# Seven products for eight in the second block's projections and in the dense layer's down products

## The chip, the cores and the metric

The kernel runs on one core of a Trainium2 chip. The metric is the device time of one execution in microseconds. The time before is 3156.32 us, the median of 3 runs (3151.3 to 3162.45).

## The reference, cut to what matters

Two blocks run one after the other on 512 tokens of width 1024, all in float32. The first block (a hybrid mixer and 16 experts) isn't touched. The second block has two layers; 16 meta tokens go ahead of the 512, so 528 rows. Each layer projects its input once, attends in a sliding window, convolves, mixes, and ends in a feed-forward part: a dense SwiGLU in the first layer, experts in the second.

```python
u = h @ w_in[i]                        # 528 x 1024 by 1024 x 3840
q, k, v = parts of u                   # 8 heads, 2 key heads, 2 value heads, of 64
y_attn = sliding_window_attention(q, k, v, sinks[i], rel_bias) @ w_attn_proj[i]
y_conv = conformer_conv(glu part of u, ...) @ w_conv_proj[i]   # 31 taps, 512 channels
mix = (sigmoid(u[..., gate a]) * y_attn + sigmoid(u[..., gate c]) * y_conv) @ w_out[i]
h = layer_norm(ALPHA * h + mix, ...)
f = (silu(h @ wg) * (h @ wu)) @ wd     # layer 0: wd is 2816 x 1024, the down products
h = layer_norm(ALPHA * h + f, ...)
```

## The kernel before

Everything is one program of blocks, each with a queue written out by hand for every engine, and semaphores between them. Layouts: `core.feat` holds the layer's input with the channel on the partition (8 chunks of 128 channels, 528 tokens), `core.hid` the rows with the token on the partition. `HALF` is 264 tokens, `P` is 128.

**The projections** (`project_and_attend`, L2351). The weights come as 31 chunks of 128 output channels in eight groups (`GROUPS`, L2108) that alternate between two buffers, `core.lead` and `w`; SP loads a group once the one before in its buffer is used (`load_behind`, L2434). A half chunk (`chunk_half`, L2460) is 8 matmuls, one for each 128 input channels, of 264 tokens into one of two banks (`ring`); ScalarE copies it out (`take`, L2563). TensorE's order: 28 half chunks for values and gates of the convolution's input (chunks 0 to 7), queries (8 to 11) and keys (12, 13; each key head is projected twice over, to lie on both halves of the partitions), then the attention's values (L2530), then 14 half chunks of the 16 gate chunks (`EARLY`). There TensorE waits until VectorE has done the convolution (L2535), makes the column sums of its layer norm (L2481), two more gate halves, the sums of squares, and enters the attention loop (L2544): for each unit (a key head and a block of queries; ten in layer 0, eight in layer 1) the scores of the next unit, transposes of the present one's weights, and the product with the values. The remaining 16 gate halves are cut into parts and put in between (`upto`, L2409), to fill the waits. VectorE's part ahead of this is to multiply values and gates (L2648) and then 124 taps, 31 for each of four chunks, two chunks in turn (L2654 to L2664).

**The dense layer** (`dense_ffn`, L2972). Its first block makes gate and up in pairs of chunks already by Strassen's method: seven products of half the inner length, from sums of weights and of inputs that VectorE makes; a product that is needed in two sums is copied out of its bank by ScalarE (L3112), and the next product is then accumulated onto the same bank. Its second block makes the down products: for each half of the 1024 output channels (weights `wd0`, then `wd1`), 22 matmuls for the 16 meta rows (L3206), and for each of four tiles of 128 tokens 22 matmuls of 512 columns (L3213). VectorE adds each to the rows (L3240), takes statistics and, in the second half, normalises; TensorE turns the rows back to channels (`norm.turn`, L2221).

**The mixing layer** (`mix_layer`, L2713) stands between and isn't changed.

Of the kernel before, what the change touches and what calls it, by code (L numbers as in the profile page):

```python
# [2107 lines left out]
GROUPS = [(0, 4), (4, 4), (8, 4), (12, 3), (15, 4), (19, 4), (23, 4), (27, 4)]  # L2108
# [242 lines left out]
def project_and_attend(core, A, i, weights, mix_in):  # L2351


    units = []
# [9 lines left out]
    PLAIN = 14  # L2364
    RINGS = 2
    EARLY = 14
    GATES = 4 * DK
    first_gate = PLAIN * 2
    CONVOLVED = CCK * CW
    with ExitStack() as ctx:  # L2370
# [9 lines left out]
        ring = core.ps(ctx, "ring", [P, RINGS, BANK])  # L2380
        ps = core.ps(ctx, "ps", [P, 2, BANK])
        pm = core.ps(ctx, "pm", [P, 2, BANK])
        ptr = core.ps(ctx, "ptr", [P, BANK])
        po = core.ps(ctx, "po", [P, BANK])
# [3 lines left out]
             "t_out o_made o_out centred squared rooted inverse normed silu").split())  # L2388
        ident, ones = core.cst[:, ID0:ID0 + P], core.cst[:, ONE0:ONE0 + P]
        eps = core.cols2[:, LAYERS * C2L:LAYERS * C2L + 1]  # L2390
        tap0 = i * C2L
        SUMS = first_gate + EARLY
        SQUARES = SUMS + 4

        def tap(c, j):
            return core.cols2[:, bass.ds(c * (CW + 3) + (tap0 + j), 1)]
# [7 lines left out]

        def gate_half(h):

            return first_gate + h + (0 if h < EARLY else 2 if h < EARLY + 2 else 4)

        def upto(u):  # L2409

            return EARLY + 2 + (GATES - EARLY - 2) * (u + 1) // len(units)

# [13 lines left out]
        with core.block() as block:  # L2426

            @block.sync
            def _(sp):
# [8 lines left out]
                load_behind(2, projected, 8)  # L2438
                load_behind(3, projected, 16)
                load_behind(4, projected, 24)  # L2440
                load_behind(5, v_made, 1)
                load_behind(6, projected, gate_half(7) + 1)
# [3 lines left out]
                load_behind(7, projected, gate_half(15) + 1)  # L2446
# [12 lines left out]
            def _(pe):  # L2459
                def chunk_half(n, g, c, half, part=None):  # L2460
                    if n >= RINGS and not part:
                        pe.wait_ge(taken, n - RINGS + 1)
                    ks = range(DK) if part is None else range(part * DK // 2, (part + 1) * DK // 2)
                    for k in ks:
                        last = pe.matmul(ring[:, n % RINGS, 0:HALF], w[g % 2][:, c, k * P:(k + 1) * P], core.feat[:, k, cols(half)],  # L2465
                                         start=k == 0, stop=k == DK - 1)
                    if ks[-1] == DK - 1:
                        last.then_inc(projected, 1)

                def gate(h, part=None):  # L2470
                    g, c = 4 + h // 8, h // 2 % 4
                    if h % 8 == 0 and not part:
                        pe.wait_ge(w_landed[g % 2], 16 * (g // 2 + 1))
                    chunk_half(gate_half(h), g, c, h % 2, part)

                def column_sums(n0, src):
                    for half in range(2):
                        n = n0 + half
                        pe.wait_ge(taken, n - RINGS + 1)
# [4 lines left out]
                def scores(u):  # L2484
# [4 lines left out]
                    for j in range(G):  # L2489
# [3 lines left out]
                        last = pe.matmul(meta(u)[:, b, c, :], q, core.k_t[rows, hk, 0:META], start=True, stop=True)  # L2493
                        if width:
                            last = pe.matmul(main(u)[:, b, c, 2 * P - width:], q, core.k_t[rows, hk, lo - width:lo], start=True, stop=True)
# [32 lines left out]
                for t, r in ROWS:  # L2528
                    for k in range(DK):
                        last = pe.matmul(ps[0:r, t // 4, (t % 4) * P:(t % 4 + 1) * P], core.feat[:, k, row_cols(t)],  # L2530
                                         w[1][:, 2, k * P:(k + 1) * P], start=k == 0, stop=k == DK - 1)
                last.then_inc(v_made, 1)
                for h in range(EARLY):
                    gate(h)
                pe.wait_ge(own, CONVOLVED)  # L2535
                column_sums(SUMS, core.conv)
                pe.wait_ge(v_out, 1)
                scores(0)
                for h in range(EARLY, EARLY + 2):
                    gate(h)  # L2540
                pe.wait_ge(squared, CCK)
                column_sums(SQUARES, sq)
                done = 2 * (EARLY + 2)
# [18 lines left out]
            def _(act):  # L2562
                def take(n, dst, f, half):  # L2563
                    act.wait_ge(projected, n + 1)
                    act.activation(dst[:, cols(half)], ring[:, n % RINGS, 0:HALF], f).then_inc(taken, 1)

                def gate(h):
                    if h // 2 >= 2 * DK - CCK - 1:
                        act.wait_ge(normed, CCK)
                    take(gate_half(h), core.gates[:, h // 2, :], ACT.Copy, h % 2)  # L2570
# [11 lines left out]
                act.wait_ge(padded, 1)  # L2582
                for n in range(first_gate):
                    c, half = divmod(n, 2)
                    if c < 4:
                        take(n, val[:, c, :], ACT.Copy, half)
                    elif c < 8:
                        take(n, glu[:, c - 4, CW - 1:], ACT.Sigmoid, half)
                    elif c < 12:
                        take(n, core.q_t[:, c - 8, :], ACT.Copy, half)  # L2590
                    else:
                        take(n, core.k_t[:, c - 12, :], ACT.Copy, half)
                act.wait_ge(v_made, 1)
                act.activation(core.v_tok[:, 0:4, :].rearrange("p t c -> p (t c)"), ps[:, 0, :], ACT.Copy)
                act.activation(core.v_tok[0:META, 4, :], ps[0:META, 1, 0:P], ACT.Copy).then_inc(v_out, 1)
                for h in range(EARLY):
                    gate(h)
# [9 lines left out]
                for h in range(EARLY, EARLY + 2):  # L2607
                    gate(h)
# [7 lines left out]
                moves, done = 0, EARLY + 2  # L2616
# [27 lines left out]
            def _(dve):  # L2644
                for c in range(CCK):
                    dve.wait_ge(taken, 2 * (4 + c) + 2)
                    g = glu[:, c, CW - 1:]
                    dve.tensor_tensor(g, g, val[:, c, :], ALU.mult).then_inc(gated, 1)  # L2648
                dve.wait_ge(gated, CCK)
                if i == 0:  # L2650
                    dve.wait_ge(core.tables.columns_in, 16)
                with dve.Fori(0, CCK // 2) as r:
                    done = r * (2 * CW)
                    for j in range(CW):  # L2654
                        for e in range(2):
                            c = r * 2 + e
                            src = glu[:, bass.ds(c, 1), :].rearrange("p a n -> p (a n)")
                            out = core.conv[:, bass.ds(c, 1), :].rearrange("p a n -> p (a n)")
                            if j == 0:
                                dve.tensor_scalar(out, src[:, 0:NTOK], tap(c, 0), tap(c, CW), ALU.mult, ALU.add).then_inc(own, 1)  # L2660
                            else:
                                dve.wait_ge(own, done + (2 * j + e - 1))
                                dve.scalar_tensor_tensor(out=out, in0=src[:, j:j + NTOK], scalar=tap(c, j), in1=out,  # L2663
# [1220 lines left out]
```

## Time and profile before

| what | value |
|---|---|
| median of 3 runs | 3156.32 us |
| the profiled execution: time | 3161.48 us |
| the profiled execution: span of its trace | 3159.7 us |
| TensorE busy | 2939.6 us (93%) |
| VectorE busy | 1140.4 us (36%) |
| ScalarE busy | 566.9 us (18%) |
| mean granted TensorE clock | 0.958 of full |

Engines in the rows: PE is TensorE, PEld its loading of weights, DVE is VectorE, ACT ScalarE, POOL GpSimd, SP SyncE. A float32 matmul stands as two records. In a timeline a row is a run of like instructions: start, length, engine, line, operation, output and inputs, shape, count, and in brackets the idle time ahead and what ended it. A granted clock of 1.00 is 2.4 GHz, 0.5 is 1.2 GHz; a value between them is a mean over a stretch.

### The profile page before, as it was taken

Reading aid. Unit: us, or ns where it says so; the run is one execution under the profiler, and the core shown is the slowest. Engines: PE = TensorE matmul, PEld = TensorE weight load, DVE = VectorE, ACT = ScalarE, POOL = GpSimd, SP = SyncE. Lnnn points to the kernel's source line nnn. Section 1 sums busy time; section 2 is a strip of 40 time slices with the busy share of each in tenths; the row PEclk is TensorE's granted clock in tenths of the full one; section 3 lists DMA queues with packets and bytes.
Section 4 is the critical chain, followed back from the end, with each engine's and each line's share of the span. In section 5 each row is a group of like instructions: output and inputs, shape, how many; then the busy total and the mean of one; then the engine's idle time right before and its main releaser. Section 6 shows DMA issues by size and latency. Waiting matters only on the chain. (4 is left out here: it accounts for less than half of the span.)

```text
span 3159.7 us, 43531 instructions
## 1 busy us (share of the span) xinstructions
PE 2939.6 (93%) x18210; PEld 1807.9 (57%) x18210; DVE 1140.4 (36%) x2083; ACT 566.9 (18%) x1340; POOL 278.4 (9%) x228
## 2 busy tenths in 40 slices
PE   8998899998969979999999999999999799999897
PEld 4544788654433327876668884478776444444343
DVE  5666666563122132921343321219213311101014
ACT  3222233222111121134011110011340000000001
POOL 0000332340000000001400000000014100000000
PEclk9999799999969988998999999999999799999998
DMA  3411000107189942211132212022120724557917
GB/s 117 109 54 44 3 17 17 54 14 278 45 337 429 427 192 64 77 57 46 75 127 80 82 68 97 0 73 87 47 95 1 281 92 162 236 201 315 407 47 288
DMA packets 79330, 414.21 MB, mean 131 GB/s; under 512 B 10515, under 2 KB 16019, under 8 KB 63428
## 3 DMA queue, kind: packets, MB, share of 16 engines
q1 hardware_dynamic: 67868, 384.75, 30.6%
q10 hardware_dynamic: 7848, 14.61, 1.9%
q0 software_dynamic: 3456, 12.58, 1.1%
q8 instruction: 118, 1.93, 0.3%
q14 instruction: 40, 0.33, 0.0%
HBM read 383.17 MB, written 28.76 MB: 130 GB/s over the span
## 5 line engine op out<-in xcount | busy, mean ns | idle before, releaser
L3593 PE MATMUL pgu<-gu,xg 128*64 128x320 f32 (+1 forms) x2560 | 396.0, 465 | 7.8 <-POOLq L3521 7.8
L3593 PEld LDWEIGHTS pgu<-gu,xg 128*64 128x64 f32 x2560 | 182.9, 138 | 205.5 <-issue 132.7
L312 PE MATMUL proj<-feat,w 128*128 128x512 f32 x576 | 254.4, 595 | 2.6 <-PEq L153 2.6
L2465 PE MATMUL ring<-feat,lead 128*128 128x264 f32 x1024 | 244.0, 398 | 3.0 <-PEq L3193 1.5
L2465 PEld LDWEIGHTS ring<-feat,lead 128*128 128x128 f32 x1024 | 198.5, 196 | 40.9 <-issue 6.3
L2465 PE MATMUL ring<-feat,w 128*128 128x264 f32 x896 | 211.1, 393 | 0.0
L3600 PE MATMUL py<-down,hm_t 128*64 128x512 f32 x880 | 200.2, 603 | 10.0 <-POOLq L3521 10.0
L2465 PEld LDWEIGHTS ring<-feat,w 128*128 128x128 f32 x896 | 170.3, 193 | 31.0 <-issue 2.7
L312 PEld LDWEIGHTS proj<-feat,w 128*128 128x128 f32 x576 | 106.7, 190 | 123.8 <-issue 123.8
L497 DVE SCALAR_TENSOR_TENSOR mixed<-padded,taps,mixed 128x512 f32<-128x512 f32 x216 | 162.4, 752 | 7.7
L2663 DVE SCALAR_TENSOR_TENSOR conv<-vg,cols,conv x240 | 163.4, 759 | 0.0
L3213 PE MATMUL po<-wd,hm 128*128 128x512 f32 x352 | 152.2, 593 | 0.0
L3662 DVE TENSOR_TENSOR hm<-sg,pgu 128x384 f32<-128x384 f32 (+1 forms) x40 | 20.8, 521 | 314.5 <-PE pgu L3593 223.9
L3600 PEld LDWEIGHTS py<-down,hm_t 128*64 128x64 f32 x880 | 61.8, 139 | 120.9 <-issue 104.1
L3213 PEld LDWEIGHTS po<-wd,hm 128*128 128x128 f32 x352 | 66.5, 190 | 83.5 <-issue 83.5
L3545 ACT ACT_TABLE_LOAD x19 | 24.4, 1283 | 459.4 <-PE pgu L3593 280.5
L3159 DVE TENSOR_TENSOR gb<-gb,pp 128x264 f32<-128x264 f32 x66 | 28.2, 429 | 174.9 <-PE pp L3071 174.9
L3071 PE MATMUL pp<-sums_x,sums_w 128*128 128x264 f32 x352 | 80.1, 386 | 0.0
L2456 POOL TENSOR_TENSOR s<-s,st 128x1088 f32<-128x1088 f32 (+2 forms) x18 | 29.1, 1619 | 518.0 <-DVE st L2704 518.0
L3071 PEld LDWEIGHTS pp<-sums_x,sums_w 128*128 128x128 f32 x352 | 66.9, 190 | 11.4
L3071 PE MATMUL pp<-feat,lead 128*128 128x264 f32 x288 | 68.7, 397 | 1.5 <-PEq L2780 1.5
L2046 DVE TENSOR_TENSOR hid_e<-act_g,pu 128x512 f32<-128x512 f32 x8 | 5.5, 688 | 177.1 <-issue 127.6
(543 smaller groups left out, 4067.1 us busy)
## 6 DMA issues: line engine op xcount, KB each, us to landing
gu<-in_moe_gu SPq DMA_DIRECT2D x16, 3072.0 KB
gu<-in_moe_gu SPq DMA_DIRECT2D x16, 2560.0 KB, 15.7
ring<-in_w_gate SPq DMA_DIRECT2D x16, 2048.0 KB, 13.4
ring<-in_w_up SPq DMA_DIRECT2D x16, 2048.0 KB, 15.0
ring<-in_w_down SPq DMA_DIRECT2D x16, 2048.0 KB, 17.4
w<-in_w_in SPq DMA_DIRECT2D x15, 2048.0 KB, 7.5
down<-in_moe_down SPq DMA_DIRECT2D x8, 3072.0 KB, 18.5
down<-in_moe_down SPq DMA_DIRECT2D x8, 2560.0 KB, 20.7
```

What stands on the lines that cost most here:

```text
L312: last = pe.matmul(proj[:, n % 2, :], w[:, g % 2, k, c * P:(c + 1) * P], core.feat[:, k, :], start=k == 0, stop=k == DK - 1)
L497: dve.scalar_tensor_tensor(out=out, in0=src[:, j:j + SEQ], scalar=taps[:, n, j:j + 1], in1=out, op0=ALU.mult, op1=ALU.add).then_inc(convol ...
L2456: pool.tensor_tensor(v, v, over(st[0:nq, u % 2, 5, :], width), ALU.mult).then_inc(scaled, 1)
L2465: last = pe.matmul(ring[:, n % RINGS, 0:HALF], w[g % 2][:, c, k * P:(k + 1) * P], core.feat[:, k, cols(half)], start=k == 0, stop=k == DK - 1)
L2663: dve.scalar_tensor_tensor(out=out, in0=src[:, j:j + NTOK], scalar=tap(c, j), in1=out, op0=ALU.mult, op1=ALU.add).then_inc(own, 1)
L3071: last = pe.matmul(bank, lhs[:, a, k * P:(k + 1) * P], rhs[:, k, :], start=begin and k == 0, stop=k == KH - 1, skip_group_check=True)
L3159: dve.tensor_tensor(dst, dst, bank, ALU.add).then_inc(added, 1)
L3213: last = pe.matmul(po[:, t, :], hm[:, f, row_cols(t)], wd[half][:, f, :], start=f == 0, stop=f == FC - 1)
L3545: act.activation(sg[:, q, 0:n], pgu[:, 2 * q, 0:n], ACT.Silu).then_inc(silu, 1)
L3593: last = pe.matmul(pgu[half(h), part, 0:n], xg[:, k, :], w[:, k, h, :], start=k == 0, stop=k == DK - 1)
L3600: last = pe.matmul(py[half(h), :], hm_t[:, c, :], down[:, c, h * BANK:(h + 1) * BANK], start=c == 0, stop=c == XC - 1)
L3662: dve.tensor_tensor(hm[:, c0:c0 + n], sg[:, q, 0:n], pgu[:, 2 * q + 1, 0:n], ALU.mult).then_inc(multiplied, 1)
```

## The change

Both places get Strassen's method with one level. A 2 by 2 block product, eight block products, becomes seven, of sums and differences (`s1` to `s4` of the one operand, `t1` to `t4` of the other). In the projections the blocks are: two chunks of output channels, two halves of the 1024 input channels, two halves of the tokens. 20 of the 30 chunks go in ten pairs (`PAIR_AT`): values and gates of the convolution, queries, keys with gate chunk 0, and gate chunks 1 to 6. The keys are projected once, and four matmuls with an identity swap the two heads into a second copy. VectorE makes the sums of weights and inputs and adds the kept products; its convolution is written out without a loop, and the new work is put between fixed taps (`BETWEEN`). ScalarE copies each product out of its bank. In layer 1 the gate halves outside the pairs leave out the meta tokens (256 columns). Three gate halves stand between the pairs and the loop (`FILLED`), 15 in the loop. The down products go in four groups of two token tiles by 512 output channels; the second half's weights are loaded in quarters into the first half's place; VectorE makes all sums, hidden ones and weights. `core.lead` holds two of the sums, and the next layer's first weights are loaded behind them.

```diff
-GROUPS = [(0, 4), (4, 4), (8, 4), (12, 3), (15, 4), (19, 4), (23, 4), (27, 4)]
+GROUPS = [(0, 4), (4, 4), (8, 4), (12, 3), (15, 4), (19, 4), (23, 4), (27, 3)]
...
+    (P1, P2, P6, P5, P7, P3, P4) = range(7)
+    PAIR_AT = [(0, 0), (0, 2), (1, 0), (1, 2), (2, 0), (2, 2), (3, 0), (4, 0), (4, 2), (5, 0)]
+    BETWEEN = {14: (2, 4), 30: (3, 5), 45: (4, 6), 62: (5, None), 70: (6, 7), 84: (None, 8), 98: (7, 9)}
...
-            return EARLY + 2 + (GATES - EARLY - 2) * (u + 1) // len(units)
+            return FILLED + (GATES - FILLED) * (u + 1) // len(units)
...
+                def pair(r):
+                    g, c = PAIR_AT[r]
+                    pe.wait_ge(w_landed[g % 2], 16 * (g // 2 + 1))
+                    if r >= 2:
+                        pe.wait_ge(copied, PRODUCTS * (r - 2) + P4 + 1)
+                    multiply(r, bank_x(r), weight(r, 0, 0), x11, True)
+                    multiply(r, bank_y(r), weight(r, 0, 1), x21, True)
+                    pe.wait_ge(w_summed, 4 * r + 2)
+                    pe.wait_ge(x_summed, 2)
+                    pe.wait_ge(copied, PRODUCTS * r + P1 + 1)
+                    multiply(r, bank_x(r), s2(r), t2, False)
+                    multiply(r, bank_z(r), s1(r), t1, True)
+                    pe.wait_ge(w_summed, 4 * r + 4)
+                    pe.wait_ge(x_summed, 4)
+                    pe.wait_ge(copied, PRODUCTS * r + P6 + 1)
+                    multiply(r, bank_x(r), s3(r), t3, False)
+                    pe.wait_ge(copied, PRODUCTS * r + P5 + 1)
+                    multiply(r, bank_z(r), s4(r), x22, False)
+                    pe.wait_ge(copied, PRODUCTS * r + P7 + 1)
+                    multiply(r, bank_x(r), weight(r, 1, 1), t4, False)
...
-                for g in range(4):
-                    pe.wait_ge(w_landed[g % 2], 16 * (g // 2 + 1))
-                    for c in range(4 if g < 3 else 2):
-                        for half in range(2):
-                            n = (g * 4 + c) * 2 + half
-                            chunk_half(n, g, c, half)
...
+                for r in range(PAIRS2):
+                    pair(r)
+                    if r == KEY_PAIR:
+                        values()
+                swap_keys()
+                gate(EARLY)
+                pe.wait_ge(v_out, 1)
+                pe.wait_ge(k_out, 2)
+                scores(0)
                 pe.wait_ge(own, CONVOLVED)
                 column_sums(SUMS, core.conv)
...
+                taps = [(q, j, 2 * q + e) for q in range(CCK // 2) for j in range(CW) for e in range(2)]
+                for n, (q, j, c) in enumerate(taps):
+                    if n in BETWEEN:
+                        sums_of, weights_of = BETWEEN[n]
+                        if sums_of:
+                            add(sums_of)
+                        if weights_of:
+                            sum_weights(weights_of)
+                    if j == 0 and c == 2 * q:
+                        gate_values(q)
...
-                    for t in range(TILES):
-                        if half:
-                            pe.wait_ge(out, t + 1)
-                        for f in range(FC):
-                            last = pe.matmul(po[:, t, :], hm[:, f, row_cols(t)], wd[half][:, f, :], start=f == 0, stop=f == FC - 1)
...
+                for part, done, dst, k, n in ((B11, P1, b11, 0, 0), (B21, P2, b21, 1, 0), (B12, P7, b12, 0, 1), (B22, P3, b22, 1, 1)):
+                    sp.wait_ge(down, DOWNS + done + 1)
+                    sp.dma_start(dst, wdv[:, k * KF:(k + 1) * KF, BANK + n * QUARTER:BANK + (n + 1) * QUARTER]).then_inc(part_in[part], 16)
+                sp.wait_ge(down, 3 * DOWNS + P5 + 1)
                 weights.load(sp)
...
+                    begin(q, P6, rows(q, 0, 1), bank_x(q))
+                    if q % 2 == 0:
+                        if q:
+                            sum_weights(half, 2)
+                        sum_weights(half, 3)
+                    begin(q, P5, rows(q, 1, 1), bank_z(q))
+                    if q % 2 == 0:
+                        small(half)
+                    if q + 1 < GROUPS2:
+                        sum_hidden(q + 1, 0, P5)
+                        sum_hidden(q + 1, 1, P6)
+                    add(q, P7, rows(q, 1, 1), bank_x(q))
```

The seven down products of a group stand in TensorE's queue in the order of `pair`, 11 matmuls each, with the wait on `out` (VectorE's reads) where `pair` waits on `copied`; the 16 meta rows stand ahead of group 0 and behind the first product of group 2.

## Rows read from the trace of the kernel before

**Rows 1.** Stages: us; PE, PEld, DVE, ACT, POOL busy; PE clock; DMA; GB/s.

```profile
1196.00:1357.00 161.00, 160.61 (x749) 137.57 (x750) 86.39 (x128) 18.05 (x45) 0.20 (x1) 0.98 0.24 84
1612.00:1890.00 278.00, 276.99 (x1232) 235.82 (x1232) 99.18 (x147) 45.75 (x112) 0.00 (x0) 0.99 0.26 97
1890.00:2063.00 173.00, 167.44 (x480) 74.07 (x480) 32.74 (x52) 6.52 (x16) 0.00 (x0) 0.99 0.14 52
2063.00:2224.00 161.00, 160.67 (x749) 137.66 (x750) 86.30 (x128) 18.03 (x44) 0.20 (x1) 0.98 0.24 89
```

**Rows 2.** Timeline of TensorE, first layer's projections to the column sums.

```profile
1196.39 31.36 PE L2465 MATMUL ring<-feat,lead 128*128 128x264 f32 x128 [1.48 <-PEq L2253]
1227.58 28.64 PE L2465 MATMUL ring<-feat,w 128*128 128x264 f32 x128
...
1298.78 9.16 PE L2530 MATMUL ps<-w,feat 128*128 128x128 f32 x80
...
1357.81 3.72 PE L2481 MATMUL ring<-conv,cst 128*128 128x264 f32 x16
```

**Rows 3.** Timeline, same stretch: the taps, and SP's load behind the last.

```profile
1258.96 40.84 DVE L2663 SCALAR_TENSOR_TENSOR conv<-vg,cols,conv  x60
...
1300.66 40.83 DVE L2663 SCALAR_TENSOR_TENSOR conv<-vg,cols,conv  x60
...
1341.52 0.37 SPq L2444 DMA_DIRECT2D vg<-in_w_mix  x1
```

**Rows 4.** Groups by form, 1400 to 2400 us: busy us, mean ns, idle before.

```profile
L3159 DVE TENSOR_TENSOR gb<-gb,pp 128x264 f32<-128x264 f32 x66 | 28.2, 429 | 174.9 <-PE pp L3071 174.9
...
L3148 DVE TENSOR_TENSOR sums_w<-sums_w,lead 128x1024 f32<-128x1024 f32 x6 | 7.4, 1225 | 0.2
```

**Rows 5.** First layer's attention loop, units 4 to 7; columns as in group 1.

```profile
1412.94:1424.85 11.91, 11.91 (x75) 8.90 (x73) 3.39 (x8) 4.94 (x15) 2.14 (x2) 1.00 0.00 0
1424.85:1438.79 13.94, 10.94 (x58) 6.68 (x56) 3.39 (x8) 4.66 (x14) 2.00 (x1) 0.82 0.01 2
1438.79:1453.14 14.35, 14.35 (x74) 10.73 (x72) 3.39 (x8) 4.82 (x15) 2.00 (x1) 0.82 0.00 0
1453.14:1467.62 14.48, 11.38 (x58) 8.15 (x57) 3.39 (x8) 10.09 (x20) 2.00 (x1) 0.76 0.01 1
```

**Rows 6.** Timeline of TensorE, second layer's attention loop, unit 0.

```profile
2241.69 3.83 PE L2465 MATMUL ring<-feat,lead 128*128 128x264 f32 x16
2245.97 0.60 PE L2506 MATMUL ptr<-cst,s 128*16 128x128 f32 x4 [0.45 <-POOL s L2456]
...
2254.98 2.17 PE L2518 MATMUL po<-pt,v_tok 16*64 16x256 f32 x8 [4.41 <-ACT pt L2627]
```

**Rows 7.** Down products: their group, then the timeline around the meta rows.

```profile
L3213 PE MATMUL po<-wd,hm 128*128 128x512 f32 x352 | 152.2, 593 | 0.0
...
1971.74 5.33 PE L3206 MATMUL pm<-wd,hm 128*16 128x512 f32 x44
...
1977.12 2.83 DVE L2962 SCALAR_TENSOR_TENSOR hid<-hid,pm 16x512 f32<-16x512 f32 x4 [3.85 <-PE pm L3206]
...
1982.38 1.27 DVE L2209 SCALAR_TENSOR_TENSOR hid<-hid,rt,gb 16x1024 f32<-16x1024 f32 x1
```

**Rows 8.** Timeline of TensorE, second layer's mixing, 256 columns.

```profile
2346.81 3.62 PE L2803 MATMUL pp<-conv,vg 128*128 128x256 f32 x16
2350.26 3.62 PE L2803 MATMUL pp<-attn,vg 128*128 128x256 f32 x16
```

**Rows 9.** Timeline of the dense gate and up stage: product and copy.

```profile
1629.78 3.72 PE L3071 MATMUL pp<-feat,lead 128*128 128x264 f32 x16
1629.98 0.39 ACT L3112 ACTIVATE gb<-pp 128x264 f32<-128x264 f32 x1 [1.39 <-PE pp L3071]
```

**Rows 10.** DMA issues: count, KB each, median us from issue to landing.

```profile
wd<-in_ffn_down SPq DMA_DIRECT2D x2, 5632.0 KB, 20.9
...
gate_w<-in_w_in SPq DMA_DIRECT2D x5, 1024.0 KB, 5.0
```

More of the change, by code:

```diff
@@ L2459, in _, with multiply @@
             def _(pe):
+                def multiply(r, bank, lhs, rhs, begin):
+                    for k in range(KH):
+                        last = pe.matmul(bank, lhs[:, k * P:(k + 1) * P], rhs[:, k, :], start=begin and k == 0,
+                                         stop=k == KH - 1, skip_group_check=True)
+                    last.then_inc(product, 1)
+                def pair(r):
+                    g, c = PAIR_AT[r]
+                    pe.wait_ge(w_landed[g % 2], 16 * (g // 2 + 1))
[16 more added lines that the diff above has]
+                    multiply(r, bank_x(r), weight(r, 1, 1), t4, False)
@@ L2569, in gate @@
                         act.wait_ge(normed, CCK)
-                    take(gate_half(h), core.gates[:, h // 2, :], ACT.Copy, h % 2)
+                    n = gate_half(h)
+                    dst = core.gates[:, h // 2, gate_cols(h % 2)]
+                    act.wait_ge(projected, n + 1)
+                    act.activation(dst, ring[:, n % RINGS, 0:dst.shape[1]], ACT.Copy).then_inc(taken, 1)
                 def soft(u):
@@ L2650, in _ @@
+                sum_weights(0, (2, 3))
+                sum_inputs(3)
+                sum_weights(1)
+                add(0)
+                sum_weights(2)
+                add(1)
+                sum_weights(3)
+                dve.wait_ge(padded, 1)
                 if i == 0:
                     dve.wait_ge(core.tables.columns_in, 16)
[L2652 to L2663, printed above, removed]
-                                                         op0=ALU.mult, op1=ALU.add).then_inc(own, 1)
@@ L3202, in _, with multiply, small @@
             def _(pe):
-                for half in range(2):
-                    pe.wait_ge(wd_in[half], 16)
+                def multiply(bank, lhs, rhs, begin):
+                    for k in range(KF):
+                        last = pe.matmul(bank, lhs[:, k, :], rhs[:, k, :], start=begin and k == 0, stop=k == KF - 1,
+                                         skip_group_check=True)
+                    last.then_inc(down, 1)
+                def small(half):
                     for f in range(FC):
-                        last = pe.matmul(pm[quarter(f % 4), half, :], hm[:, f, row_cols(TILES)], wd[half][:, f, :],
+                        last = pe.matmul(banks[half][quarter(f % 4), :], hm[:, f, row_cols(TILES)], wd[:, f, :],
@@ L3217, in _ @@
+                norm.turn(pe, TILES - 1, banks)
                 norm.turn(pe, TILES, banks)
@@ L3228, in _, with rows, begin, add @@
             def _(dve):
-                for half in range(2):
+                def rows(q, a, n):
+                    lo = q // 2 * BANK + n * QUARTER
+                    return core.hid[:, q % 2 * 2 + a, lo:lo + QUARTER]
+                def begin(q, j, h, bank):
+                    dve.wait_ge(down, DOWNS * q + j + 1)
+                    dve.scalar_tensor_tensor(out=h, in0=h, scalar=ALPHA, in1=bank, op0=ALU.mult, op1=ALU.add).then_inc(out, 1)
+                def add(q, j, h, bank):
+                    dve.wait_ge(down, DOWNS * q + j + 1)
+                    dve.wait_ge(out, DOWNS * q + j)
+                    dve.tensor_tensor(h, h, bank, ALU.add).then_inc(out, 1)
@@ L3235, in _ @@
                         norm.normalize(dve, 0, taken=len(norm.rows) + 1)
[L3236 to L3245 removed]
+                dve.wait_ge(wd_in[0], 16)
```

359 lines of the change are left out of this document (277 added, 82 removed).

## The prediction

> **What bounds the kernel now.** I read the table of stages first [rows 1]. In the first layer's projections (1196 to 1357 us) TensorE is busy for 160.61 of 161 us, in the dense layer's gate and up products for 276.99 of 278, in its down products for 167.44 of 173, and the second layer's projections (2063 to 2224) repeat the first layer's. So in every stage that the change touches TensorE is the bound, and a matmul taken out is time taken out, as long as the engines that now have to feed the products keep up. Next the timeline of TensorE [rows 2]. A float32 matmul stands in the trace as two records: 128 records of 264 columns take 28.64 us, so 0.2225 us a record. The first 128 of the stage take 31.36 us: it starts at the lower clock, which costs 2.7 us and stays. The down products are 352 records of 512 columns, 152.2 us with the ends of their eight runs, some 150.9 in issue (0.4287 each) [rows 7].
>
> Then VectorE. In the projections it has one large job, the convolution: 124 taps, 60 of them in 40.84 us, so 0.679 us a tap [rows 3]. It is done at 1341.5, and TensorE arrives at the column sums that wait for it at 1357.8 [rows 2, 3]: 16.3 us of slack. The change spends just this slack.
>
> **The change part by part, projections.** Before, two chunks (256 output channels) over both halves of the tokens are 2 x 2 x 8 = 32 matmuls. After, 7 products of 4 are 28. Ten pairs save 40 matmuls. The keys were projected twice (two duplicated chunks, now one real chunk): 16 matmuls less. The swap of the two key heads adds 4. Net 52 matmuls, 104 records x 0.2225 = 23.1 us a layer. By place: ahead of the column sums stood 28 + 14 half chunks (672 records); now stand 560 of the pairs, 8 of the swap and 16 of one gate half: 88 fewer, 19.6 us. The missing 16 records (3.56 us) come out of the attention loop, where gate halves fill waits. The second layer's remaining 18 gate halves get 256 columns for 264: 16 records in 3.45 us [rows 8] for 3.56, 1.9 us less in all.
>
> Is each product fed? A product is 8 records, 1.78 us. Four of the seven wait for ScalarE to copy out the bank that they write again, always with one other product between. The trace has such a copy in the dense stage: the next product starts at 1629.78, the copy at 1629.98, and takes 0.39 [rows 9]. With a tenth back to TensorE that is 0.7 us of 1.78. So I cost the 70 copies a layer at nothing; what hides each is the product between.
>
> VectorE's new work: a sum of 512 elements isn't in the trace; 1024 take 1.225 us, 264 take 0.43 [rows 4], and the line between gives 0.68. With the wait for the one before I take 0.72, four to a pair, 2.9 us. Four sums of inputs (1056 elements) are 1.27 each. Three additions of 264 are 1.1 us a pair. From the stage's start: weights 0, inputs, weights 1, additions 0, weights 2, additions 1 end at 27.2 (pair 1's sixth product ends at 26.1, and VectorE stands behind it), weights 3 at 30.1; the sigmoids of pair 1 and two multiplications make 31.6. From there 124 taps (84.2), six additions (6.6), six sets of weights (17.3) and the second gating (1.4) end at 141.1. TensorE arrives at 2.7 + 10 x 12.46 + 9.1 (values) + 1.8 (swap) + 3.6 (gate) + 0.3 = 142.1. The margin shrinks from 16.3 us to about 1. I take the wait as 0; each microsecond of VectorE beyond one comes onto the path, twice. Each pair's weights are summed 3 to 8 us ahead of TensorE's need; the loads keep some 8 us from issue to landing [rows 10] and are issued at least 20 ahead, so SP's queue costs nothing.
>
> **The attention loop.** The first layer's ten units share 15 gate halves for 16. A unit with two halves takes 11.91 us, all of it TensorE; a unit with one takes 13.94 and leaves 14.35 for its follower, since its 3.0 us of idle bring the granted clock from 1.00 to 0.82; another one takes 14.48 with a clock of 0.76 [rows 5]. So a unit with one half costs 2.6 to 4.5 us more than one with two, though it does 3.56 less. Before, units 5 and 7 have one; by the new count units 4, 6 and 8 have. One more: +3.5 us, where a plain sum has -3.56. In the second layer the half is taken from unit 0. There TensorE works until 2245.5, waits, and then waits for ScalarE again until 2254.98 [rows 6]; that end is set by VectorE and ScalarE, so nothing is saved and TensorE idles from 2241.7. Fourteen halves follow, as before. First layer: -19.6 + 3.5 = -16.1. Second: -19.6 - 1.9 + 0.9 for a possible drop of the clock = -20.6.
>
> **The down products.** 4 groups x 7 x 11 matmuls of 256 columns, 616 records. At 3.45 us for 16 [rows 8], 0.2157 each, 132.9 us for 150.9: -18.0. The row for 256 columns is half of that for 512, so narrower products cost nothing that the rows show. The Trainium skill (TensorE: Matmul & The Clock Gate, Why this matters for your kernels) speaks against such a split, advising to keep all dimensions at 512 or more for 85% of peak; the fixed 2.5 ns a matmul that its gap formula has would make an estimate of 0.7 us for the 264 records that the stage gets more, so -17.3 for -18.0; the trace has no such difference that I could read.
>
> The rows of 16 tokens stay (5.33 us a half [rows 7]). VectorE now adds each product (0.42), sums hidden blocks (1408 elements, 1.65 at 1024 elements' rate, four to a group) and weights (2816 elements, 3.11, four to a half). I walked through its order against TensorE's, whose product is 4.75 us. Group 0 holds: the seventh needed read (P7) is done 1.7 us before TensorE wants it. Group 2 doesn't. From its start TensorE ends P6 at 19.5 and wants P7's sum read at 33.8. VectorE has after P6: 0.6, two weight sums 6.2, P5 0.4, the 16 rows with their normalisation 6.5 (1977.12 to 1983.65 [rows 7]), two hidden sums 3.3, P7's addition 0.4, done at 37.0. A stall of 3.3 us. Idle of 3 us brought the clock down above [rows 5], at 5 us lost over two units; at even odds and more I take 2.7. The quarter loads (1408 KB) aren't in the trace; 1024 KB land in 5.0 us and 5632 in 20.9 [rows 10], so 5 to 7 us, and TensorE wants the last quarter 9.5 after its issue: 0, at worst 3. The end of the stage keeps its shape. Sum -18.0 + 3.3 + 2.7 = -12.0.
>
> **The sum.** -16.1 - 20.6 - 12.0 = -48.7 us against a span of 3159.7 (time 3161.5). The median of the runs is 3156.3, 5 us below the profiled execution, and I take the difference off it: 3107.6, say 3108.
>
> **The rivals.** (a) The forecast; its own range is 3097 to 3122, from the bounds of the loop (0 to +6), of the stall with its clock (0 to 9), and a few us of conv wait.
> (b) All is covered: no stall, no drop of the clock, the missing half is won: -23.1 - 25.0 - 18.0 = -66, less the anchored unit's 3.6: 3094. Against it: units of one half already cost more than they save [rows 5].
> (c) VectorE becomes the bound of both projections. It decides from 1 us of lateness. Ahead of the convolution's end stand some 70 new instructions; at 0.13 us more for each (waits between dependent sums that I took at 0.03) it is 9 us late, and such an idle brings the clock down for 5 more: 2 x (8 + 5) = 26, so 3134. For it: the margin is 1 us of 141. Against: VectorE's taps lose their loop and its register work, which could give back some hundredths each.
> (d) Slower than before: ScalarE's copies. If the way product, copy, next product takes over 1.78 us, four products a pair wait. At 2.4 us the saving is gone (4 x 20 pairs x 0.62 = 50); I price the rival at 2.6 us, 4 x 20 x 0.82 = 66 more, so 3174. Rows 9 have 0.7, with longer only behind the two sigmoids and their table load.
> (e) The bank cycling. Products that change banks leave small gaps, and the clock swings: at the 0.8 of the attention units [rows 5] the 125 us of pairs would take 31 more in each layer: 3170. Against it: the dense gate and up stage runs the same seven products at a granted clock of 0.99 [rows 1]. The Trainium skill (TensorE: Matmul & The Clock Gate, A second HAM failure mode: psum-queue depth-cycling) describes this effect; by its rule the pairs would swing, and here the dense stage disagrees.
>
> **Chances.** (a) 0.62, (b) 0.16, (c) 0.15, (d) 0.04, (e) 0.03. A measurement of this kernel tells about 0.3%, 9.5 us, from no change. (a), (b) and (c) lie beyond it at their prices; a deep (c) could come inside, 0.02. Faster 0.91, same 0.02, slower 0.07. The range takes in (b) and (c) up to its price: 3091 to 3134.
>
> **What would show it.** In the projections TensorE busy without a gap over 1 us until the column sums, some 142 us after the stage's start, and the last tap within 2 us of it. In the first layer's loop drops of the clock at three units. In the down stage 616 records near 0.216 us and one gap of some 3 us ahead of the last product of the third group. Wrong would be: gaps between products inside a pair (d), a clock under 0.95 in the pairs (e), or an idle of more than 3 us ahead of the column sums (c).

## The result, and the profile after

The changed kernel takes 3103.66 us (median of 4 runs, 3101.01 to 3104.66) against 3156.63 for the kernel before on the same chip: a ratio of 0.9825, 95% interval 0.9807 to 0.9844, or 53 us less (by the interval 49 to 61). In a second set of runs it was 3101.62 (3099.45 to 3103.51) against 3159.63, ratio 0.9812 (0.9798 to 0.9827). The forecast was 3108, with 3091 to 3134 around it. The two profiled executions differ by 60.5 us (3159.7 and 3099.2 us of span), more than the first pair of medians; a part of it is a slower first attention loop in the one trace of before, as the experiments show. Medians here are of fast runs: one of the six runs of the last kernel below, with both edits, took 4799.43 us at a granted clock of 0.578 and is left out.

The table of stages after, in the columns of [rows 1]. Its stages are those of [rows 1] in the same order, with the first layer's attention loop (the second line) put in:

```profile
1200.00:1341.00 141.00, 140.74 (x662) 119.98 (x663) 127.38 (x199) 31.84 (x79) 0.20 (x1) 0.98 0.24 82
1341.87:1468.17 126.30, 109.61 (x639) 81.58 (x633) 36.76 (x94) 53.14 (x157) 14.85 (x10) 0.97 0.07 26
...
1590.40:1867.00 276.60, 276.50 (x1232) 235.47 (x1232) 99.19 (x146) 45.27 (x111) 0.00 (x0) 0.99 0.26 97
1867.00:2026.00 159.00, 150.37 (x744) 124.63 (x744) 87.65 (x96) 6.75 (x16) 0.00 (x0) 0.99 0.16 57
2026.00:2168.00 142.00, 141.95 (x672) 120.91 (x673) 127.37 (x199) 32.22 (x80) 0.20 (x1) 0.98 0.25 90
```

TensorE is still busy without a gap in the projections, now for 141 and 142 us where it was 161. VectorE goes from 86.4 to 127.4 us of work in that stretch, 90% of it: the slack is spent. The gate and up stage is the same as before.

The timeline at the end of the first layer's projections, TensorE's column sums and VectorE's last 14 taps, and behind them the additions of pair 8:

```profile
1329.33 9.59 DVE L2825 SCALAR_TENSOR_TENSOR conv<-vg,cols,conv 128x528 f32<-128x528 f32 x14
1338.84 1.11 DVE L2787 TENSOR_TENSOR gates<-gates,attn 128x264 f32<-128x264 f32 x3
...
1341.87 3.83 PE L2589 MATMUL pp<-conv,cst 128*128 128x264 f32 x16
```

The taps end at 1338.9, and TensorE arrives 2.95 us later with no wait; in [rows 2, 3] it was 16.3 us.

Three units of the first layer's attention loop, in the same columns; the first and third have one gate half, the second has two. They answer to [rows 5]:

```profile
1396.73:1408.35 11.62, 8.62 (x58) 5.85 (x56) 3.39 (x8) 4.66 (x14) 2.13 (x2) 1.00 0.01 1
1408.35:1420.25 11.90, 11.90 (x74) 8.89 (x72) 3.39 (x8) 4.94 (x15) 2.00 (x1) 1.00 0.00 0
1420.25:1431.88 11.63, 8.62 (x59) 5.86 (x57) 3.39 (x8) 4.66 (x14) 2.00 (x1) 1.00 0.01 1
```

The idle is the 3.0 us of [rows 5]. The clock stays at 1.00, though, and a unit with one half takes 11.6 us instead of 13.9.

The down products, at their third group: TensorE, then VectorE's queue behind P5 (the 16 meta rows with their normalisation from 1966.37, two hidden sums, P7's addition):

```profile
1964.12 9.66 PE L3400 MATMUL pd<-wd,sums_h 128*128 128x256 f32 x44
1976.76 6.67 PE L3400 MATMUL pd<-sums_t,hm 128*128 128x256 f32 x22 [2.98 <-DVE hid L3471]
```

```profile
1966.37 2.82 DVE L3126 SCALAR_TENSOR_TENSOR hid<-hid,pd 16x512 f32<-16x512 f32 x4
...
1972.82 1.61 DVE L3489 TENSOR_TENSOR lead<-hm 128x1408 f32<-128x1408 f32 x1
1974.53 1.63 DVE L3489 TENSOR_TENSOR lead<-lead,hm 128x1408 f32<-128x1408 f32 x1
1976.19 0.42 DVE L3471 TENSOR_TENSOR hid<-hid,pd 128x256 f32<-128x256 f32 x1
```

The wait is 2.98 us, and the product behind it takes 6.67 us where the others take 4.91. The granted clock from 1976.7 to 1983.4 us is 0.75, so half of that time is at 1.2 GHz.

### The profile page after: what moved, and what is told of

It is laid out like the page before. It is cut to its first block and busy times, and to the rows that moved or that the text cites. A ratio compares the mean times of both kernels' runs of the same rounds, so it can differ in the third digit from the quotient of the medians.

```text
span 3099.2 us, 43532 instructions
## 1 busy us (share of the span) xinstructions
PE 2865.6 (92%) x18266; PEld 1810.5 (58%) x18266; DVE 1279.5 (41%) x2275; ACT 593.9 (19%) x1408; POOL 278.0 (9%) x228
## 3 DMA queue, kind: packets, MB, share of 16 engines
q8 instruction: 119, 1.95, 0.3%
## 5 line engine op out<-in xcount | busy, mean ns | idle before, releaser
L2825 DVE SCALAR_TENSOR_TENSOR conv<-vg,cols,conv 128x528 f32<-128x528 f32 x240 | 164.3, 761 | 0.0
L3237 PE MATMUL pp<-sums_x,sums_w 128*128 128x264 f32 x352 | 80.1, 386 | 0.0
L2570 PE MATMUL pp<-feat,w 128*128 128x264 f32 (+1 forms) x320 | 78.0, 391 | 0.0
L2524 PE MATMUL pp<-sums_x,sums_w 128*128 128x264 f32 x320 | 74.5, 386 | 0.0
L3237 PEld LDWEIGHTS pp<-sums_x,sums_w 128*128 128x128 f32 x352 | 66.9, 190 | 11.4
L2524 PEld LDWEIGHTS pp<-sums_x,sums_w 128*128 128x128 f32 x320 | 60.8, 190 | 10.4
L2570 PEld LDWEIGHTS pp<-feat,w 128*128 128x128 f32 x320 | 59.4, 194 | 11.3 <-issue 2.6
L2570 PE MATMUL pp<-feat,lead 128*128 128x264 f32 (+1 forms) x256 | 65.7, 405 | 0.0
L3835 POOL DMA_INDIRECT gu<-moe_out,place x8 | 7.8, 981 | 640.3 <-POOLq L3831 638.2
## 6 DMA issues: line engine op xcount, KB each, us to landing
down<-in_moe_down SPq DMA_DIRECT2D x8, 3072.0 KB, 18.6
down<-in_moe_down SPq DMA_DIRECT2D x8, 2560.0 KB, 20.6
```

Of the source, the lines that this page charges most:

```text
L2524: last = pe.matmul(bank, lhs[:, k * P:(k + 1) * P], rhs[:, k, :], start=begin and k == 0, stop=k == KH - 1, skip_group_check=True)
L2570: last = pe.matmul(ring[:, n % RINGS, 0:src.shape[1]], w[g % 2][:, c, k * P:(k + 1) * P], src, start=k == 0, stop=k == DK - 1)
L2825: dve.scalar_tensor_tensor(out=out, in0=glu[:, c, j:j + NTOK], scalar=tap(c, j), in1=out, op0=ALU.mult, op1=ALU.add).then_inc(own, 1)
L3237: last = pe.matmul(bank, lhs[:, a, k * P:(k + 1) * P], rhs[:, k, :], start=begin and k == 0, stop=k == KH - 1, skip_group_check=True)
```

## The experiments

For each kernel the timelines give the length of the stages (from the first matmul of one to the first of the next). This table is worked out from them. "Both edits" are the reordered down products and the other filling of the loop ("fill"), both described below; "to sums" is from a layer's first product to its column sums, "loop" from there to the mixing layer. Shifts of the stages ahead of the projections (1194 to 1202 us in all kernels, none changed there) are left out.

| kernel | to sums, 1st | loop, 1st | down | to sums, 2nd | loop, 2nd |
|---|---|---|---|---|---|
| before | 161.4 | 132.8 | 172.6 | 161.5 | 118.5 |
| before, second trace | 160.2 | 128.0 | 172.6 | 161.5 | 118.5 |
| down products alone | 161.5 | 126.9 | 158.2 | 161.6 | 118.6 |
| after | 141.6 | 126.3 | 158.2 | 142.6 | 115.8 |
| after, second trace | 140.4 | 128.1 | 158.2 | 142.7 | 115.9 |
| projections alone | 140.8 | 129.1 | 171.7 | 142.7 | 115.8 |
| down reordered | 141.7 | 126.4 | 154.2 | 141.3 | 112.5 |
| fill alone | 141.6 | 119.3 | 158.2 | 142.6 | 113.8 |
| both edits | 141.8 | 120.1 | 154.2 | 142.8 | 113.8 |
| both edits, second trace | 141.3 | 119.2 | 154.2 | 141.2 | 113.0 |
| late taps | 150.2 | 128.9 | 158.2 | 149.9 | 116.8 |
| two extra copies | 141.0 | 124.9 | 158.2 | 143.0 | 115.8 |
| four extra copies | 160.6 | 124.9 | 158.2 | 161.4 | 112.5 |

### The two halves of the change, each alone

The changed kernel with `dense_ffn` of before:

```diff
 def dense_ffn(core, A, w_in, weights):
...
-        wd = wd0
-        sums_t = sb("sums_t", 3, KF, QUARTER)
...
+        wd1 = sb("wd1", FC, BANK)
+        wd = (wd0, wd1)
...
```

> The changed kernel with the down products of before (and their two halves of weights loaded whole). Theory: the parts add up, since TensorE bounds each stage and none hands work to the next. The two traces give the projections with attention -26.3 us in the first layer and -21.5 us in the second, 47.8 in all, and the down stage -14.4; so the ratio to before should be 0.985 (about 3109 us). The forecast's own terms (-16.1 and -20.6) would make it 0.988 (3120). Rival: what the first layer's attention loop gained in the trace (6.5 us) is a drop of the clock that happened to fall in the profile of before and not in that of after; then the profile here shows the loop again anywhere between 126 and 133 us, with as many drops as it happens to have. The last tap should end some 2.9 us ahead of TensorE.

Measured: 3115.47 us, ratio 0.9864 (0.9849 to 0.9878), 43 us less.

The kernel before with `dense_ffn` of after, the same edit the other way round:

```diff
 def dense_ffn(core, A, w_in, weights):
...
-        wd1 = sb("wd1", FC, BANK)
-        wd = (wd0, wd1)
...
+        wd = wd0
+        sums_t = sb("sums_t", 3, KF, QUARTER)
...
```

> The kernel before with the down products of after alone. Theory: -14.4 us by the traces (172.6 to 158.2 us from the first meta matmul to the next layer's first), ratio 0.9954, one wait of about 3 us ahead of the last product of the third group, matmul records 0.216 us apart. The forecast's term was -12.0 (0.9962). Rival: a part of the gain of both changes comes only together; then this is under 8 us.

Measured: 3143.41 us, ratio 0.9960 (0.9947 to 0.9972), 12.6 us less by the ratio and 14.5 between the medians. The two ratios multiply to 0.9824, and the changed kernel has 0.9825. So the parts add up within the intervals, which are 4 to 5 us to each side. In the traces the down stage is 14.4 us shorter. The interval of the runs (9 to 17 us) can't tell this from the forecast's 12.0.

The first layer's loop takes 129.1 us in the first of these kernels and 126.3 in the first trace of the changed kernel, with the same code. The end of the loop in its trace, unit 8 with one half:

```profile
1451.05 0.66 PE L2614 MATMUL pp<-cst,s 128*128 128x128 f32 x4 [2.33 <-ACT pt L2746]
1451.55 2.95 PE L2570 MATMUL pp<-feat,w 128*128 128x264 f32 x8
1454.42 3.02 PE L2626 MATMUL pp<-pt,v_tok 16*64 16x256 f32 x12
1457.38 2.91 PE L2570 MATMUL pp<-feat,w 128*128 128x264 f32 x8
```

The wait is the 2.33 us that the changed kernel has at the same place; here the clock drops behind it, and eight records take 2.95 us for 1.95.

### The kernel before, a second time

There is no edit: it is the kernel before as it stands, for another trace of its loop.

> The kernel before, unchanged, for a second trace of it. If the first layer's attention loop is 132.8 us again (column sums to mixing) with the clock falling in two places, the drops belong to its order of work; if it is nearer to 123 to 128, they come by chance and the comparison of two traces overstates the loop's gain.

Measured: 3153.60 us in one run, and a loop of 128.0 us for 132.8. Three rows for the loop follow, in the columns of [rows 1]: of the first trace, of this one, and of the kernel with the down products alone, whose loop is the same code.

```profile
1357.81:1490.61 132.80, 120.55 (x657) 89.67 (x656) 35.74 (x91) 53.39 (x158) 14.86 (x10) 0.91 0.05 17
```

```profile
1354.21:1482.21 128.00, 115.11 (x657) 85.69 (x656) 35.72 (x91) 53.51 (x158) 14.87 (x10) 0.95 0.05 17
```

```profile
1360.94:1487.84 126.90, 114.61 (x657) 85.56 (x656) 35.70 (x91) 53.54 (x158) 14.87 (x10) 0.96 0.05 17
```

Idle is 12.2, 12.9 and 12.3 us: the same. What differs is the granted clock, 0.91, 0.95 and 0.96, and with it the busy time of the same 657 matmul records. So the drops at units 5 and 7 that I read in [rows 5] don't belong to the order of work. The profile of before had caught a loop with more of them than the two others.

### The down products reordered

```diff
                     begin(q, P5, rows(q, 1, 1), bank_z(q))
-                    if q % 2 == 0:
-                        small(half)
+                    if q == 0:
+                        small(0)
                     if q + 1 < GROUPS2:
                         sum_hidden(q + 1, 0, P5)
                         sum_hidden(q + 1, 1, P6)
                     add(q, P7, rows(q, 1, 1), bank_x(q))
+                    if q == 2:
+                        small(1)
```

> The changed kernel with one thing moved: in the third group of the down products VectorE adds the seventh needed product (P7) and makes the next group's first two sums ahead of the 16 meta rows and their normalisation. Theory: the 2.98 us wait of TensorE ahead of P4 goes, with the 1.8 us that the drop of the clock behind it cost; the turn of the next rows may now wait 0.6 us. So 4 us less than the changed kernel: 3100 us, ratio 0.981 to before. Rival: VectorE's chain is only shifted and the wait comes back at the two turns of the fourth group; then no change, 3104.

Measured: 3093.26 us, ratio 0.9795 (0.9783 to 0.9808). The stage goes from 158.2 to 154.2 us, the expected 4.0. The timeline of TensorE at the same place has neither the wait nor the slow product, and the turns behind it don't wait either:

```profile
1960.82 9.66 PE L3400 MATMUL pd<-wd,sums_h 128*128 128x256 f32 x44
1970.31 4.91 PE L3400 MATMUL pd<-sums_t,hm 128*128 128x256 f32 x22
1975.15 0.67 PE L2227 MATMUL pd<-cst,hid 16*128 16x16 f32 x8
```

The medians are 10 us apart. Of the rest, 4.6 us stand in the second layer, whose start and loop are shorter in this trace with the same code and at a higher granted clock (0.97 for 0.96 in the loop); what remains isn't accounted for by the stages touched. The two were measured in separate sets of runs, and the intervals allow a difference of 0 to 19 us, so the stage's 4.0 is what is shown.

### The convolution made late

24 additions are put in front of tap 100 in both layers (a scratch tile and a semaphore with them).

```diff
+                    if n == 100:
+                        for e in range(24):
+                            if e:
+                                dve.wait_ge(spared, e)
+                            dve.tensor_tensor(spare[:, :], core.cst[:, 0:HALF], core.cst[:, 0:HALF], ALU.add).then_inc(spared, 1)
                     if n in BETWEEN:
```

> The changed kernel with 24 additions of 264 elements on VectorE put in front of tap 100 of both layers, each waiting for the one before: some 0.45 us each, 11 us more ahead of the convolution's end. Theory: the last tap ended 2.95 us ahead of TensorE in the trace, so TensorE now waits 8 us ahead of the column sums, and the clock drops behind the wait, for 0 to 4 us more: 16 to 24 us over both layers, 3120 to 3128 for the changed kernel's 3104. Rival: the forecast's margin of 1 us was right and the 2.95 is partly pipeline; then 10 us of wait a layer. Second rival: the slack isn't what binds and something else hides it; then under 5 us in all.

Measured: 3122.27 us, 18.6 more than the changed kernel's first median; ratio to before 0.9881 (0.9865 to 0.9896). TensorE's wait, from the table of waits of the first layer's stretch, and of the second's:

```profile
PE pp L2591 <- DVE conv L2832: 8.1, 1, 8.1
```

```profile
PE pp L2591 <- DVE conv L2832: 7.2, 1, 7.2
```

The additions on VectorE, and the column sums on TensorE behind the first wait:

```profile
1324.99 11.17 DVE L2818 TENSOR_TENSOR spare<-cst 128x264 f32<-128x264 f32 x24
```

```profile
1352.52 6.84 PE L2591 MATMUL pp<-conv,cst 128*128 128x264 f32 x16 [8.13 <-DVE conv L2832]
```

The 24 additions hold the next tap back by 11.1 us. Less the 2.95 of margin that is 8.1, the wait. In the second layer of the trace of after the last tap ends 3.83 us ahead of the column sums (2164.83 and 2168.66), and 11.1 less 3.83 is 7.3, for a wait of 7.2. So the margins are what the trace of after shows, and here each microsecond of VectorE beyond them is one of TensorE. The column sums behind the wait take 6.84 us for 3.83. This is the forecast's rival (c), reached by 3 to 4 us of VectorE more, not by 1.

### ScalarE's copies made longer

Two or four extra copies of the bank ahead of each copy in the pairs, each waiting for the one before; here with four.

```diff
                     act.wait_ge(product, PRODUCTS * r + j + 1)
+                    for e in range(4):
+                        if extra[0]:
+                            act.wait_ge(spared, extra[0])
+                        act.activation(spare[:, :], bank, ACT.Copy).then_inc(spared, 1)
+                        extra[0] += 1
                     act.activation(dst, bank, f).then_inc(copied, 1)
```

> The changed kernel with two extra copies of the same bank on ScalarE ahead of each product's copy in the pairs, each waiting for the one before (about 0.42 us each): the way from product to next product on the same bank becomes 1.5 us for 0.7. Theory: the product between takes 1.78 us and hides it, so no change but at the two pairs with sigmoids: 0 to 4 us. Rival (the forecast's d): the way is longer than read off, near 1.78 already; then 4 waits a pair of up to 0.8 us, 20 to 60 us more.

Measured with two: 3098.61 us, ratio 0.9807 (0.9792 to 0.9822), no slower than the changed kernel, and 141.0 us to the column sums for 141.6. The stretch in its trace:

```profile
1199.50:1340.50 141.00, 140.83 (x673) 119.64 (x673) 127.42 (x199) 78.58 (x220) 0.10 (x1) 0.99 0.25 83
```

ScalarE works 78.58 us of 141 there, for 31.84, and it costs nothing.

> As the one with two extra copies, with four: the way is 2.4 us, and ScalarE has 7 x 2.1 = 14.5 us of work in a pair of 12.46. Theory: each of four products in a pair waits some 0.6 us, 2.5 us a pair, 50 us in 20 pairs: about 3150, and with gaps of 0.6 us between products the granted clock stays at 1.00. Rival (the forecast's e): small gaps at each change of bank bring the clock down; then it is under 0.95 in the pairs and the loss is well over 60 us.

Measured with four: 3136.04 us, ratio 0.9927 (0.9911 to 0.9942), and 160.6 us to the column sums. The stretch and, from the timelines of TensorE and ScalarE, pair 2:

```profile
1199.00:1359.00 160.00, 148.36 (x663) 117.21 (x664) 127.67 (x199) 129.11 (x359) 0.09 (x1) 0.98 0.24 85
```

```profile
1235.56 3.80 PE L2527 MATMUL pp<-sums_x,sums_w 128*128 128x264 f32 x16 [2.24 <-ACT attn L2675]
1239.69 2.02 PE L2527 MATMUL pp<-sums_x,w 128*128 128x264 f32 x8 [0.34 <-ACT attn L2675]
```

```profile
1237.61 1.66 ACT L2673 ACTIVATE spare<-pp 128x264 f32<-128x264 f32 x4 [0.37 <-PE pp L2527]
1239.16 0.39 ACT L2675 ACTIVATE attn<-pp 128x264 f32<-128x264 f32 x1
```

The four extra copies and the copy end 2.0 us after the first of them starts. A pair now takes 14.2 to 14.5 us for 12.46, which is the 19 us more a layer. ScalarE alone doesn't set this pace. In the pair that starts at 1245.62 us (14.18 us long) it works 12.47 us and waits three times for a product, 0.30 to 0.37 us each, while TensorE waits for its copies. So the whole way, product, copy, next product, now sets it. I had expected 50 us from four waits of 0.6 a pair. Most of those in the trace are 0.25 to 0.4 us (one is 2.24), and the measured 32 also has the second layer's loop in it, which came out at 112.5 for 115.8 us.

With two extra copies the way is about 1.5 us instead of 0.7, by adding the two, and costs nothing, so the copies have the room that the forecast gave them. And the granted clock with four is 0.98 in this stretch with some 12 us of small gaps, the same as without them; from 1235.56 to 1302.71 us, within pairs 2 to 6, it is 1.00. Gaps of a few tenths between products on changing banks don't bring it down here. That ends rival (e). The Trainium skill (TensorE: Matmul & The Clock Gate, A second HAM failure mode: psum-queue depth-cycling) reports a clock that swings for a bf16 kernel that cycles through banks with 512 columns. No run here shows it for float32 products of 1.78 us.

### The gate halves dealt out otherwise

```diff
         def upto(u):
-            return FILLED + (GATES - FILLED) * (u + 1) // len(units)
+            return FILLED + -(-(GATES - FILLED) * (u + 1) // len(units))
```

First on top of the reordered down products:

> The kernel with the down products reordered, and the 15 gate halves of the attention loop dealt out rounded up: unit 0 gets two for one in both layers, and the last unit one for two. Theory: unit 0's end is set by VectorE and ScalarE, so its idle takes the half for nothing, and a later unit has a half less: 2 to 4 us less in the first layer's loop and in the second's (126.3 and 112.5 to 115.8 us before), and a drop of the clock less; 3086 to 3090 for 3093. Rival: the units with one half take as long as those with two (11.6 for 11.9 us), so a half moved away saves 0.3 us; what is won at unit 0 is lost at the last; 3093.

Measured: 3088.34 us, ratio 0.9770 (0.9757 to 0.9783), against 0.9795 (0.9783 to 0.9808) without this edit, and a loop of 120.1 us for 126.4. Then alone, beside the changed kernel and the kernel with both edits:

> The changed kernel with only the gate halves dealt out rounded up. Theory: 3 to 6 us less in the first layer's loop (120 to 123 us), 0 to 2 in the second's; 3 to 6 us less than the changed kernel on this chip. Rival: the gain seen together with the reordered down products was a drop of the clock less; then the loop is 124 us or more here and the time is the changed kernel's.

> The changed kernel again, beside the next two on the same chip, and with a second trace. If the drops of the clock in the attention loops come by chance, the first layer's loop is again somewhere between 124.9 and 129.1 us, and the stages ahead of it don't differ (141 to 143 us to the column sums, 158.2 us for the down stage). Median 3101 to 3106.

> Both edits, again, on the chip of the two others: 4 us for the down products, 3 to 6 for the fill, 7 to 14 less than the changed kernel here, since phases of the clock shift as well. Ratio to before 0.977 to 0.979.

Measured on one chip: the changed kernel 3101.62 us, ratio 0.9812 (0.9798 to 0.9827); the fill alone 3098.05, 0.9793 (0.9777 to 0.9809); both edits 3088.11 (median of five), 0.9776 (0.9761 to 0.9791). The loops' rows, changed kernel and fill alone:

```profile
1338.54:1466.65 128.11, 112.82 (x639) 83.42 (x633) 36.76 (x94) 53.13 (x157) 14.85 (x10) 0.95 0.07 26
```

```profile
1343.30:1462.60 119.30, 108.63 (x638) 81.32 (x633) 36.76 (x94) 52.96 (x157) 14.85 (x10) 0.97 0.08 28
```

Idle, the length less TensorE's busy time, falls from 15.3 to 10.7 us (16.7 in the first trace of after). The waits for ScalarE's `pt` fall from 10.5 to 6.8 us. All three loops with the fill (119.2 to 120.1) lie below all seven of the changed kernel's order (124.9 to 129.1), and their idle (10.7 to 10.9) below that of all seven (15.0 to 16.7). So this is no drop of the clock alone. In the time of the kernel the fill alone isn't told apart (the intervals overlap); both edits together are 11 us (by the ratios) to 13.5 us (by the medians) faster than the changed kernel on that chip, with intervals that don't overlap. It is the fastest version found.

## Why the prediction was right

**The bound and the saving ahead of the column sums.** Right to 1 us. 19.6 us a layer were forecast; the traces have 161.4 and 160.2 before against 141.6 and 140.4 after in the first layer, 161.5 against 142.6 in the second. TensorE arrives 141.6 us after the start, for 142.1.

**VectorE's margin.** The step was right in its direction and 2 us too low. The walk gave the last tap at 141.1 us; it was 138.7 (2.95 us of slack, not 1). A sum of 512 came out at 0.69 us with 0.72 from one to the next, as taken, and a tap at 0.68; the two unrolled tap rows confirm that writing the loop out gave back nothing. The first taps started at 31.0 for 31.6, and a good part of the rest is in the six inserted groups: three additions and four sums take 3.8 us (1240.32 to 1244.13) for the 4.0 taken. The second layer's margin was 3.83. The late taps show that both count as they are read.

**The copies** at nothing: right, and shown with three copies in the place of each.

**The attention loop.** Here the step failed. I put +3.5 us on the first layer's loop, from [rows 5]: a unit with one half costs 2.6 to 4.5 us more than one with two. That price held a drop of the clock as if it belonged to the 3.0 us of idle. Three traces of the order before (132.8, 128.0, 126.9) and six of the order after (126.3, 128.1, 129.1, 126.4, 124.9, 124.9; the one with the late taps left out) show much the same idle for each order (12.2 to 12.9, and 15.0 to 16.7) and drops in different places. Of the three drops that I named for the new order (units 4, 6 and 8) the second trace of after has two, the projections alone have one, and the four others have none. Without one, the units take 11.6 and 11.9 us, so the missing half is worth nothing rather than costing 3.5: idle rises from 12 us to between 15 and 17 (one more unit with 3.0, and a wait of 1.51 in unit 7) and eats its 3.56. The means, 129.2 and 126.6, differ by 2.6 us, for a large part through the drops. So the term is near 0 to -3, not +3.5, and the first layer gains 20 to 23 us, not 16.1. In the second layer's unit 0 the idle became longer, as described: a wait of 4.21 us ahead of the first transposes where it was 0.45, and 9.5 us of idle in the loop for 7.2. Its loop is 2.7 us shorter, of which the narrower gates are 1.6 by their width, and the rest isn't taken apart. That layer gains 21.5 us in the traces for 20.6.

**The down products.** 616 records near 0.216 us (44 in 9.50), the wait of the third group 2.98 us for 3.3 forecast, in the place and from the queue named; the drop behind it cost 1.8 for 2.7. That VectorE's queue is the cause of the wait is shown by the reordering. The quarter loads kept nobody waiting. The end of the stage didn't quite keep its shape: from the turn of the last tile to the next layer's first product it takes 7.0 us for 8.15, which the forecast had at no change. In all 14.4 us in the traces, and 12.6 by the ratio of the runs, for 12.0.

One reading in this part was wrong. The forecast said that the trace has no fixed cost of a narrower record that one could read. It has: from the starts of single records at full clock, 512 columns take 0.4292 us, 264 take 0.2225 and 256 take 0.2158. Two of 256 are 2.5 ns longer than one of 512, which is the amount that the forecast had as an estimate. But its -18.0 comes from rows of both widths and holds this already (352 x 0.4292 less 616 x 0.2158 is 18.1), so the -17.3 beside it counts it twice.

**The sum.** -48.7 forecast, -53 and -58 in the two comparisons. The stages of the traces, as means over those with the same code, add up to some 59: 20.1 and 2.6 in the first layer, 14.4 in the down products, 18.9 and 2.7 in the second. The term of the loop (6 us off) and that of the down products (2.4) both had too little gain, so no large error made up for another. The time came out inside the range because the range was wider than these. The 60.5 us between the profiled executions overstate the change: the profile of before had a first loop in which TensorE was busy 5 to 6 us longer, at a lower granted clock, than in the two other traces of that order.

**The rivals.** (b) isn't what happened: the missing half isn't won, and a stall stays. (c) would have needed 3 to 4 us more of VectorE a layer. (d) and (e) are excluded by the longer copies.

## What to carry to other kernels

Where one engine is busy without a gap, count its records from the trace and write out the queue of the engine that is to feed it, instruction by instruction: here this gave the arrival at the next wait to half a microsecond, and a 3 us stall in its right place, in a stage where VectorE's work went from 32.7 to 87.7 us. Price a unit with a wait in it from two or more traces before a drop of the clock goes into its cost: idle is a property of the order, a drop behind 3 us of it isn't there every time. And after such a change look for what stands in a feeder's queue ahead of the one result that the bound engine wants (the meta rows ahead of P7), and for idle that is anchored elsewhere (unit 0), and move work out of the first and into the second.

## What the runs showed of the hardware that I had not expected

The granted clock behind the same 2.33 us wait in the same code was once 1.00 (eight records in 1.95 us) and once lower (2.95 us). Over all 13 traces the first layer's loop has 27 such waits of 2.33 us for `pt`, and the clock falls behind 6 of them. It has 6 of 3.1 us, and the clock falls behind 5. Over nine traces of two orders of the loop this moves its length by 6 us in one and 4 us in the other, 0.1 to 0.2% of the kernel. Between the two traces of the kernel before, the loop has 4.8 of the 7.9 us of difference; how much of the spread of the other runs it makes up, their single times can't show. Some 12 us of gaps in 160, spread over tenths of a microsecond between products, left the granted clock at 0.98.
